# Layer norm in a two-block transformer kernel: the row normalization by ScalarE instead of VectorE

## The chip, the cores and the metric

The kernel runs on one core of a Trainium2 chip, in one launch. The metric is the device time of that launch in microseconds (us). A core has five engines that run side by side and meet only at semaphores: TensorE (PE in the profile; PEld is its weight load), VectorE (DVE), ScalarE (ACT), GpSimd (POOL) and SyncE (SP, which issues most of the DMAs). Each engine takes its own instructions in program order.

## The reference, cut to what matters

Two blocks of two layers each work on 256 tokens of 1024 features in float32. In the first block each layer is a mixer and an MLP, and each of these four sublayers ends in a layer norm, whose rows feed the next projection:

```
def layer_norm(x, g, b):
    mu = mean(x, -1);  var = mean(square(x - mu), -1)
    return (x - mu) * rsqrt(var + 1e-5) * g + b

for layer in range(2):
    shift, scale, gate = ada_modulation(c, ada_w[layer, 0], ada_b[layer, 0])
    h = x * (1 + scale) + shift
    y = mixer(h)                                   # layer 0: windowed + sparse, layer 1: block attention
    x = layer_norm(ALPHA * x + gate * y, ln_g[layer, 0], ln_b[layer, 0])
    shift, scale, gate = ada_modulation(c, ada_w[layer, 1], ada_b[layer, 1])
    h = x * (1 + scale) + shift
    y = square(relu(h @ w1)) @ w2
    x = layer_norm(ALPHA * x + gate * y, ln_g[layer, 1], ln_b[layer, 1])
```

The second block (neighbourhood attention, full attention, a per-layer gate, RMS norms) has no layer norm.

## The kernel before, in words

The 256 tokens lie as T = 2 tiles of 128 rows, called t = 0 and t = 1. A weight tile is 128 x 2048 floats (1 MB) and lands in one of five slots `raw`. Each product is done in a split form: ScalarE rounds the tile to the high part `w_hi` (L1293, three slots, plus `w_spare`), VectorE subtracts to get the low part `w_lo` (L1851, written over `raw`), and TensorE does three matmuls per chunk, with `w_lo`, `w_hi` and the low part of the activations. The activations are split likewise into `ht_hi` and `ht_lo`. ScalarE's and VectorE's parts of a weight tile are issued some tiles ahead (`split_high`, `split_low`, up to `it["ahead"]`).

A function `make_plan` writes one list of items by hand, and all engines walk through this list in the same order, each doing its share of an item. So the place of an item in the list is its place in every engine's queue that has a share in it. A DMA into a `raw` slot waits for the `tile_done` of the tile that was there.

A layer norm of sublayer s is made so, once for each t (item `ln`, from `norm_ln(s, t)`):
- VectorE's eviction of the last projection (`y_ln`, L2109 to L2112) adds gate and residual into `u` and takes statistics, in two column halves.
- `ln` on VectorE (L2137 to L2140): aggregate, add eps, a reciprocal square root in nine one-column instructions (`rsqrt_one`, L1872 to L1877), and then L2140, which normalizes all 1024 columns of `u[:, t, :]` in place and raises `rows_ready`.
- TensorE transposes the rows (item `turn_rows` of the next sublayer, from `across`, L1684) once `rows_ready` allows it. The transposed rows get gain, norm bias and modulation in one step by ScalarE (L1357) and are rounded to `ht_hi` (L1361), then VectorE takes `ht_lo` (L1856). For the second half of t = 1 VectorE does all of it (L2066, L2070, L1856).

Around a layer norm the list reads, in `entered` (before an MLP; s is the MLP's number, so its norm is s - 1) and in `halves` (before a mixer's projections) alike:

```
norm_ln(s - 1, 0)                    # placed before the last projection tiles of t = 1
across(s, 0, ...)                    # transposes of t = 0
norm_ln(s - 1, 1)
ada_tiles(2, 7)                      # in halves it stands before norm_ln(s - 1, 1)
part(0, 0) or first(0, 1, ts=(0,))   # first weight tile of the next projection, t = 0; ahead = 1
across(s, 1, ...)                    # transposes of t = 1
part(0, 1) or first(1, 0, ts=(0,))   # second weight tile, t = 0
```

So there are four such places (norms 0 to 3), with one `ln` of t = 0 and one of t = 1 in each. The item after `ln` of t = 1 carries, on ScalarE and VectorE, the split of the second weight tile.

Of the kernel before, what the change touches and what calls it, by code (L numbers as in the profile page):

```python
# [33 lines left out]
ALU = mybir.AluOpType  # L34
ACT = mybir.ActivationFunctionType
AX = mybir.AxisListType.X

P = 128
S = 256
T = S // P  # L40
# [902 lines left out]
def block_kernel(nc, R, out, toeplitz):  # L943
# [3 lines left out]
    with ExitStack() as ctx:  # L947
        def sb(name, shape, dt=F32):
            return ctx.enter_context(nc.sbuf_tensor(name, shape, dt))

        def sem(name):
            return ctx.enter_context(nc.semaphore(name))
# [3 lines left out]
        u = sb("u", [P, T, D])  # L956
# [23 lines left out]
        gain = sb("gain", [P, 2, HD])  # L980
        stats = sb("stats", [P, T, 2, 6])
        meanvar = sb("meanvar", [P, T, 2])
        ssq = sb("ssq", [P, T, 2])
        rms = sb("rms", [P, 4, 2, T])
        small = sb("small", [P, 3, 24])
        bits = sb("bits", [P, 24], U32)
        rstd = sb("rstd", [P, 24])
# [66 lines left out]
        squares_ready = sem("squares_ready")  # L1054
        key_squares = sem("key_squares")
        rows_ready = sem("rows_ready")
        silu_ready = sem("silu_ready")
        early_affine = sem("early_affine")
        affine_ready = sem("affine_ready")
# [90 lines left out]
        def head_cols(mode, t):  # L1150

            return P * (t + 1) if mode in ("causal", "window", "sparse", "index") else S
# [5 lines left out]
        def turned_view(mode, p2):  # L1158

            n = P * len(turned_blocks(mode))  # L1160
            return probs_t[:, p2, :, :].rearrange("p b s -> p (b s)")[:, 0:n], n
# [107 lines left out]
        def _(act):  # L1269
# [25 lines left out]
            def squares(t, n):  # L1295
                nc.scalar.activation(junk[:, :], x[:, t, n * 512:(n + 1) * 512], ACT.Square,
                                     accum_out=ssq[:, t, n:n + 1]).then_inc(ssq_ready, 1)
                squared[0] += 1
                act.wait_ge(ssq_ready, squared[0])
# [9 lines left out]
            for it in plan:  # L1309
                kind = it["kind"]  # L1310
# [38 lines left out]
                elif kind == "turn_rows" and it["engine"] == "act":  # L1349
# [5 lines left out]
                    for c in range(4):  # L1355
                        k = it["a"] + c
                        ins = nc.scalar.activation(full[:, b % 4, c * P:(c + 1) * P], bank[b][:, c * P:(c + 1) * P], ACT.Identity,  # L1357
                                                   scale=aff[:, it["s"], 0, k:k + 1], bias=aff[:, it["s"], 1, k:k + 1])
# [28 lines left out]
                elif kind in ("tokens", "hidden", "up_tokens", "turn_hidden", "evict"):  # L1387
# [24 lines left out]
                    elif end[0] in ("tok", "silu"):  # L1412
                        c0, scale, width = end[1:4]
# [38 lines left out]
                elif kind == "resid" and it["s"] == 3 and it["t"] == T - 1:  # L1452
                    for t in range(T):
                        act.wait_ge(first_rows, T + t + 1)
                        for n in range(2):
                            squares(t, n)

                elif kind == "index":
                    for j in range(2):
                        b, _ = it["banks"][j]  # L1460
                        act.wait_ge(index_scores, 2 * it["p"] + j + 1)
                        if it["p"]:
                            act.wait_ge(index_used, 2 * it["p"] + j - 1)
                        for t in range(T):
                            m = head_cols("index", t)
                            ins = nc.scalar.activation(biased[:, j, t, 0:m], bank[b][:, t * S:t * S + m], ACT.Relu)
                        ins.then_inc(bank_free[b], 1)

                elif kind == "scores":
                    mode, g = it["mode"], it["g"]  # L1470
                    for j in range(2):
                        b, _ = it["banks"][j]
                        r = g % PAIRS_HELD
                        if mode == "window":
                            act.wait_ge(band_ready, g + 1)
                        else:
                            act.wait_ge(negmax_ready, 2 * (g - BANDED) + j + 1)
                        if g >= 2:
                            act.wait_ge(probs_turned, 2 * (g - 2) + j + 1)
                        if mode == "window":  # L1480
                            hh = it["heads"][j][4]
                            nc.scalar.activation(sink_exp[:, r, :, j], nmx[:, r, :, j], ACT.Exp, bias=sinks[:, 0, hh:hh + 1])
                        for t in range(T):
                            m = head_cols(mode, t)
                            src = biased[:, j, t, :] if mode == "near" else bank[b][:, t * S:t * S + m]
                            by = q_norm[:, t, it["heads"][j][4]:it["heads"][j][4] + 1] if mode == "full" else -1.0
                            ins = nc.scalar.activation(probs[:, g % 2, j, t, 0:m], src, ACT.Exp, bias=nmx[:, r, t, j:j + 1], scale=by,
                                                       accum_out=sums[:, r, t, j:j + 1])
                        ins.then_inc(probs_ready if mode == "near" else bank_free[b], 1)

                elif kind == "split_out":
                    act.wait_ge(tile_done, it["projected"] + 1)
                    for b, used in it["after"]:
                        act.wait_ge(bank_free[b], used)
                    a = it["a"]
                    nc.scalar.activation(ht_hi[:, a:a + 2, :], out_turned[:, a:a + 2, :], ACT.Copy).then_inc(high_copied, 1)

                elif kind == "values" and it["mode"] in TURNED_OUT:
                    b, _ = it["banks"][0]
                    act.wait_ge(head_out, 2 * it["g"] + 2)  # L1500
                    nc.scalar.activation(out_turned[:, it["heads"][0][4] // 2, :], bank[b][:, 0:S], ACT.Copy).then_inc(bank_free[b], 1)

                elif kind == "scale" and it["mode"] in NORMED_BY_SCALAR:
                    g = it["g"]
                    act.wait_ge(sums_turned, g + 1)
                    for j in range(2):
                        for t in range(T):
                            rows = probs[:, g % 2, j, t, 0:head_cols(it["mode"], t)]
                            ins = nc.scalar.activation(rows, rows, ACT.Copy, scale=rs[:, g % PAIRS_HELD, t, j:j + 1])
                        ins.then_inc(normed, 1)  # L1510

                elif kind == "probs":
                    g = it["g"]
                    for j in range(2):
                        b, _ = it["banks"][j]
                        act.wait_ge(probs_turned, 2 * g + j + 1)
                        if g >= 1:
                            act.wait_ge(head_out, 2 * g + j - 1)
                        dst, n = turned_view(it["mode"], j)
                        nc.scalar.activation(dst, bank[b][:, 0:n], ACT.Copy).then_inc(bank_free[b], 1)  # L1520
# [299 lines left out]
        def _(dve):  # L1820
            steps = [0]

            def link(ins):

                steps[0] += 1
                ins.then_inc(dve_step, 1)
                dve.wait_ge(dve_step, steps[0])
# [41 lines left out]
            def rsqrt_one(y, v):  # L1869

                t = small[:, 1, 0:1]
                link(nc.vector.tensor_scalar(bits[:, 0:1], v.bitcast(U32), 1, None, ALU.logical_shift_right))  # L1872
                link(nc.vector.tensor_scalar(y.bitcast(U32), bits[:, 0:1], -1.0, RSQRT_MAGIC, ALU.mult, ALU.add))
                for less in (3.0, 12.0, 768.0):
                    link(nc.vector.scalar_tensor_tensor(t, y, v, y, ALU.mult, ALU.mult))
                    link(nc.vector.scalar_tensor_tensor(y, t, -less, y, ALU.add, ALU.mult))
                link(nc.vector.tensor_scalar(y, y, -1.0 / 8192, None, ALU.mult))  # L1877
# [59 lines left out]
            for it in plan:  # L1937
                kind = it["kind"]
# [34 lines left out]
                elif kind == "columns":  # L1973
# [4 lines left out]
                    bias = vec[:, 3 * KD * it["s"] + at:3 * KD * it["s"] + at + KD]  # L1978
                    dst, src = mod[:, it["s"], at:at + KD], bank[b][:, 0:KD]
                    if it["how"] == "rows":  # L1980
                        dst, bias = (v.rearrange("p (c i) -> p i c", c=2) for v in (dst, bias))
# [153 lines left out]
                elif kind == "ln":  # L2135
                    t = it["t"]
                    link(nc.vector.bn_aggr(meanvar[:, t, :], stats[:, t, :, :]))  # L2137
                    link(nc.vector.tensor_scalar(small[:, 0, 0:1], meanvar[:, t, 1:2], LN_EPS, None, ALU.add))
                    rsqrt_one(rstd[:, 0:1], small[:, 0, 0:1])
                    nc.vector.tensor_scalar(u[:, t, :], u[:, t, :], meanvar[:, t, 0:1], rstd[:, 0:1], ALU.subtract, ALU.mult).then_inc(rows_ready, 1)  # L2140
                    dve.wait_ge(rows_ready, it["rows"])

                elif kind == "resid":

                    t = it["t"]
# [117 lines left out]
                elif kind == "topk":  # L2263

                    for r in range(it["first"], it["first"] + 4):
                        t = r // 8
# [58 lines left out]
                elif kind == "scale":  # L2325
# [10 lines left out]
                    for j in range(2):  # L2336
                        for t in range(T):
                            rows = probs[:, g % 2, j, t, 0:head_cols(mode, t)]
# [75 lines left out]
```

## Time and profile before

| | |
|---|---|
| median of 3 runs (lowest, highest) | 1054.5 us (1053.75, 1055.5) |
| the profiled execution: its time, its span | 1052.61 us, 1050.8 us |
| TensorE busy, its mean granted clock | 978.2 us (93%), 0.98 of full speed |
| VectorE busy | 720.1 us (69%) |
| ScalarE busy | 543.6 us (52%) |
| GpSimd busy | 49.2 us (5%) |
| DMA | 204.85 MB, mean 195 GB/s |
| the chain that ended last, by engine | PE 66%, DVE 17%, ACT 7%, DMA 6%, issue 3% |

The span runs from the first to the last instruction; the time has 1.8 us around it. Busy time is that of matmuls whose ends are modelled. "Issue" is time in which the profile shows nothing that was waited for. In a timeline a row is: start in us, duration in us, engine, line, operation, output <- inputs, shape, count, and in brackets the idle time before it with what ended it.

### The profile page before, as it was taken

The numbers are of one execution on the slowest core, as the hardware profiler recorded it, in microseconds if no ns is written. First come the engines' busy times: TensorE is split into PE (matmuls) and PEld (weight loads), VectorE is DVE, ScalarE is ACT, GpSimd is POOL, SyncE is SP. The second block draws the span as 40 slices with busy tenths as digits, with TensorE's granted clock in tenths as the row PEclk, the third lists the DMA queues.
The fourth block names the chain that finished last, engine by engine and source line by source line (L and its number), as shares of the span: only waits on it lengthen the run. The fifth ranks groups of instructions, "written<-read, shape, count | busy, mean of one in ns | idle before, by whom it ended". The sixth has DMA issues, their size and how long they took to land.

```text
span 1050.8 us, 14669 instructions
## 1 busy us (share of the span) xinstructions
PE 978.2 (93%) x5692; PEld 792.5 (75%) x5692; DVE 720.1 (69%) x1113; ACT 543.6 (52%) x869; POOL 49.2 (5%) x39
## 2 busy tenths in 40 slices
PE   6886998999999989999899999989999999998995
PEld 2663666989898866777699989877788887875684
DVE  3488668777776587565885554478654778797775
ACT  3367725544453253555355455435565746656662
POOL 0000003200000000000071100000000000000000
PEclk9999999999999989999999999999999999999998
DMA  9747476879897468332689776554434346551041
GB/s 350 245 145 295 161 240 214 287 258 341 298 328 261 160 238 294 127 118 64 200 269 254 209 234 188 183 190 132 149 121 130 121 141 200 187 174 61 32 160 40
DMA packets 106931, 204.85 MB, mean 195 GB/s; under 512 B 3488, under 2 KB 37680, under 8 KB 106864
## 3 DMA queue, kind: packets, MB, share of 16 engines
q1 hardware_dynamic: 103808, 193.25, 54.8%
q0 software_dynamic: 3056, 10.67, 3.5%
q8 instruction: 46, 0.75, 0.3%
q14 instruction: 21, 0.17, 0.0%
HBM read 202.76 MB, written 1.15 MB: 194 GB/s over the span
## 4 chain that ended last, share of the span: by engine, by line
PE 66%; DVE 17%; ACT 7%; DMA 6%; issue 3%; SPq 1%; ACTq 0%; DVEq 0%
PE bank L1672 13%; PE bank L1674 13%; PE bank L1673 13%; DVE w_lo L1851 5%; PE bank L1726 5%; PE bank L1728 4%; PE bank L1727 4%; DMA raw<-in_mlp_w 3%; PE bank L1747 2%; ACT w_hi L1293 2%; PE bank L1769 2%; DMA raw<-in_ada_w 2%; DMA raw<-in_ab_w_in 1%; PE bank L1574 1%; PE bank L1814 1%
## 5 line engine op out<-in xcount | busy, mean ns | idle before, releaser
L1851 DVE TENSOR_TENSOR w_lo<-raw,w_hi 128x2048 fp32r<-128x2048 f32 (+2 forms) x134 | 308.6, 2311 | 154.5 <-ACT w_hi L1293 153.4
L1293 ACT ACTIVATE w_hi<-raw 128x2048 fp32r<-128x2048 f32 (+2 forms) x134 | 248.5, 1857 | 131.3 <-PE bank L1674 69.2
L1672 PE MATMUL bank<-w_lo,ht_hi 128*128 128x512 f32 (+1 forms) x544 | 218.4, 401 | 12.5 <-DVE w_lo L1851 7.8
L1674 PE MATMUL bank<-w_hi,ht_lo 128*128 128x512 f32 (+1 forms) x528 | 206.4, 391 | 0.0
L1673 PE MATMUL bank<-w_hi,ht_hi 128*128 128x512 f32 (+1 forms) x528 | 206.1, 390 | 0.0
L1672 PEld LDWEIGHTS bank<-w_lo,ht_hi 128*128 128x128 f32 x544 | 103.7, 191 | 41.8 <-issue 21.4
L1726 PE MATMUL bank<-ht_hi,w_lo 128*128 128x256 f32 x448 | 127.5, 285 | 2.4 <-DVE w_lo L1851 2.4
L1727 PE MATMUL bank<-ht_lo,w_hi 128*128 128x256 f32 x448 | 126.8, 283 | 0.0
L1728 PE MATMUL bank<-ht_hi,w_hi 128*128 128x256 f32 x448 | 126.8, 283 | 0.0
L1674 PEld LDWEIGHTS bank<-w_hi,ht_lo 128*128 128x128 f32 x528 | 100.5, 190 | 21.3
L1673 PEld LDWEIGHTS bank<-w_hi,ht_hi 128*128 128x128 f32 x528 | 101.0, 191 | 18.8
L1672 PE MATMUL bank<-w_lo,hid_hi 128*128 128x512 f32 x256 | 102.0, 399 | 0.0
L1673 PE MATMUL bank<-w_hi,hid_hi 128*128 128x512 f32 x240 | 94.6, 394 | 0.0
L1674 PE MATMUL bank<-w_hi,hid_lo 128*128 128x512 f32 x240 | 94.4, 393 | 0.0
L1726 PEld LDWEIGHTS bank<-ht_hi,w_lo 128*128 128x128 f32 x448 | 85.9, 192 | 5.1 <-issue 5.0
L1727 PEld LDWEIGHTS bank<-ht_lo,w_hi 128*128 128x128 f32 x448 | 86.0, 192 | 0.2
L1728 PEld LDWEIGHTS bank<-ht_hi,w_hi 128*128 128x128 f32 x448 | 86.0, 192 | 0.0
L1672 PEld LDWEIGHTS bank<-w_lo,hid_hi 128*128 128x128 f32 x256 | 48.8, 191 | 10.5 <-issue 0.5
L1357 ACT ACTIVATE full<-bank,aff 128x128 f32<-128x128 f32 x48 | 18.0, 455 | 71.0 <-PE bank L1684 71.0
L1673 PEld LDWEIGHTS bank<-w_hi,hid_hi 128*128 128x128 f32 x240 | 45.9, 191 | 9.9 <-issue 0.5
L1674 PEld LDWEIGHTS bank<-w_hi,hid_lo 128*128 128x128 f32 x240 | 45.8, 191 | 9.7
L1856 DVE TENSOR_TENSOR hid_lo<-full,hid_hi 128x512 fp32r<-128x512 f32 x32 | 24.1, 760 | 33.5 <-ACT hid_hi L1410 33.4
(244 smaller groups left out, 1334.2 us busy)
## 6 DMA issues: line engine op xcount, KB each, us to landing
raw<-in_mlp_w SPq DMA_DIRECT2D x64, 1024.0 KB, 6.0
raw<-in_ada_w SPq DMA_DIRECT2D x44, 1024.0 KB, 5.3
raw<-in_a_w_in SPq DMA_DIRECT2D x16, 1024.0 KB, 5.3
raw<-in_c_w_in SPq DMA_DIRECT2D x12, 1024.0 KB, 5.4
raw<-in_b_w_in SPq DMA_DIRECT2D x10, 1024.0 KB, 5.1
raw<-in_ple_w_gate SPq DMA_DIRECT2D x8, 1024.0 KB, 5.0
raw<-in_ab_w_in SPq DMA_DIRECT2D x4, 1024.0 KB, 9.8
tok<-in_ada_w SPq DMA_DIRECT2D x4, 1024.0 KB, 12.8
```

What stands on the lines that cost most here:

```text
L1293: nc.scalar.activation(split_parts(n)[0], raw_tile(t), ACT.Copy).then_inc(high_done, 1)
L1357: ins = nc.scalar.activation(full[:, b % 4, c * P:(c + 1) * P], bank[b][:, c * P:(c + 1) * P], ACT.Identity, scale=aff[:, it["s"], 0, k:k ...
L1672: nc.tensor.matmul(dst, a_hi[:, c, rows], lo[:, k, :], start=it["first"] and k == 0, stop=False)
L1673: nc.tensor.matmul(dst, a_hi[:, c, rows], hi[:, k, :], start=False, stop=False)
L1674: mm = nc.tensor.matmul(dst, a_lo[:, c, rows], hi[:, k, :], start=False, stop=it["last"] and k == it["kc"] - 1)
L1726: nc.tensor.matmul(dst, lo[:, k, cols], ht_hi[:, k, :], start=k == 0, stop=False)
L1727: nc.tensor.matmul(dst, hi[:, k, cols], ht_lo[:, k, :], start=False, stop=False)
L1728: mm = nc.tensor.matmul(dst, hi[:, k, cols], ht_hi[:, k, :], start=False, stop=k == KD - 1)
L1747: done.append(nc.tensor.matmul(bank[b][:, t * S:t * S + m], qkt[part, qc, t * P:(t + 1) * P], qkt[part, kc, 0:m], start=True, stop=not masks))
L1769: mm = nc.tensor.transpose(bank[b][:, i * P:(i + 1) * P], probs[:, g % 2, j, t, k * P:(k + 1) * P], ident)
L1851: nc.vector.tensor_tensor(lo, raw_tile(split[n]), hi.bitcast(F32), ALU.subtract).then_inc(low_done, 1)
L1856: nc.vector.tensor_tensor(lo, v, hi.bitcast(F32), ALU.subtract).then_inc(split_done, 1)
```

## The change

VectorE no longer normalizes the rows. After the reciprocal square root, which now has a column of `rstd` for each t, it computes `less` = -(mean x rstd), one value per token, and raises a new semaphore `norm_ready`. ScalarE gets a share in the item `ln`: it waits for `norm_ready` and computes `u` = rstd x `u` + `less` in place, as one activation (Identity) with a scale and a bias per partition, and raises `rows_ready`. The list is the same.

```
@@ ScalarE
+                elif kind == "ln":
+                    t = it["t"]
+                    act.wait_ge(norm_ready, T * it["s"] + t + 1)
+                    nc.scalar.activation(u[:, t, :], u[:, t, :], ACT.Identity, scale=rstd[:, t:t + 1], bias=less[:, t, :]).then_inc(rows_ready, 1)
@@ VectorE
                     link(nc.vector.bn_aggr(meanvar[:, t, :], stats[:, t, :, :]))
                     link(nc.vector.tensor_scalar(small[:, 0, 0:1], meanvar[:, t, 1:2], LN_EPS, None, ALU.add))
-                    rsqrt_one(rstd[:, 0:1], small[:, 0, 0:1])
-                    nc.vector.tensor_scalar(u[:, t, :], u[:, t, :], meanvar[:, t, 0:1], rstd[:, 0:1], ALU.subtract, ALU.mult).then_inc(rows_ready, 1)
-                    dve.wait_ge(rows_ready, it["rows"])
+                    rsqrt_one(rstd[:, t:t + 1], small[:, 0, 0:1])
+                    nc.vector.scalar_tensor_tensor(less[:, t, :], meanvar[:, t, 0:1], -1.0, rstd[:, t:t + 1], ALU.mult, ALU.mult).then_inc(norm_ready, 1)
+                    dve.wait_ge(norm_ready, T * it["s"] + t + 1)
```

ScalarE's queue at the first layer norm (s = 0), before. The four L1357 and the L1361 handle transposed rows, `w_hi` is the split of a weight tile:

```order
L1293 ACTIVATE w_hi<-raw 128x2048 [waits tile_done,raw_in2]
L1357 ACTIVATE full<-bank,aff 128x128 [waits split_done,affine_ready,job_done]
L1357 ACTIVATE full<-bank,aff 128x128 x3
L1361 ACTIVATE ht_hi<-full 128x4x128 [waits bank_free4]
L1357 ACTIVATE full<-bank,aff 128x128 [waits split_done,affine_ready,job_done]
L1357 ACTIVATE full<-bank,aff 128x128 x3
L1361 ACTIVATE ht_hi<-full 128x4x128 [waits bank_free5]
L1293 ACTIVATE w_hi<-raw 128x2048 [waits tile_done,raw_in4]
L1357 ACTIVATE full<-bank,aff 128x128 [waits split_done,affine_ready,job_done]
```

The same place in the changed kernel:

```order
L1295 ACTIVATE w_hi<-raw 128x2048 [waits tile_done,raw_in2]
L1496 ACTIVATE u<-u,less,rstd 128x1024 [waits norm_ready]
L1359 ACTIVATE full<-bank,aff 128x128 [waits split_done,affine_ready,job_done]
L1359 ACTIVATE full<-bank,aff 128x128 x3
L1363 ACTIVATE ht_hi<-full 128x4x128 [waits bank_free4]
L1359 ACTIVATE full<-bank,aff 128x128 [waits split_done,affine_ready,job_done]
L1359 ACTIVATE full<-bank,aff 128x128 x3
L1363 ACTIVATE ht_hi<-full 128x4x128 [waits bank_free5]
L1496 ACTIVATE u<-u,less,rstd 128x1024 [waits norm_ready]
L1295 ACTIVATE w_hi<-raw 128x2048 [waits tile_done,raw_in4]
L1359 ACTIVATE full<-bank,aff 128x128 [waits split_done,affine_ready,job_done]
```

Two instructions are new, one for each t; the second stands ahead of a `w_hi` which the transposed rows of t = 1 follow. The other three layer norms read the same.

VectorE's queue at the `ln` of t = 1 of the same norm, before:

```order
L1877 TENSOR_SCALAR rstd<-rstd 128x1 [waits dve_step]
L2140 TENSOR_SCALAR u<-u,meanvar,rstd 128x1024 [waits dve_step]
L1851 TENSOR_TENSOR w_lo<-raw,w_hi 128x2048 [waits high_done,rows_ready]
L1856 TENSOR_TENSOR ht_lo<-full,ht_hi 128x4x128 [waits high_copied]
L2066 TENSOR_SCALAR full<-bank,aff 128x128 [waits job_done]
```

And in the changed kernel:

```order
L1884 TENSOR_SCALAR rstd<-rstd 128x1 [waits dve_step]
L2147 SCALAR_TENSOR_TENSOR less<-meanvar,rstd 128x1 [waits dve_step]
L1858 TENSOR_TENSOR w_lo<-raw,w_hi 128x2048 [waits high_done,norm_ready]
L1863 TENSOR_TENSOR ht_lo<-full,ht_hi 128x4x128 [waits high_copied]
L2073 TENSOR_SCALAR full<-bank,aff 128x128 [waits job_done]
```

One instruction takes the place of another there; nothing is moved. TensorE's, GpSimd's and SyncE's queues hold the same instructions in the same order.

## Rows read from the trace of the kernel before

**Rows 1.** Part 1 of the page: busy us, share, instructions.

```profile
PE 978.2 (93%) x5692; PEld 792.5 (75%) x5692; DVE 720.1 (69%) x1113; ACT 543.6 (52%) x869; POOL 49.2 (5%) x39
```

**Rows 2.** Waits: who for whom, us in total, times, longest.

```profile
PE bank L1684 <- DVE u L2140: 4.4, 6, 2.1
...
PE bank L1698 <- DVE w_lo L1851: 1.7, 2, 1.2
```

**Rows 3.** Timeline of VectorE at the first norm.

```profile
160.41 0.81 DVE L2140 TENSOR_SCALAR u<-u,meanvar,rstd 128x1024 f32<-128x1024 f32 x1
...
165.62 1.37 DVE L1856 TENSOR_TENSOR ht_lo<-full,ht_hi 128x512 fp32r<-128x512 f32 x2
...
169.06 0.15 DVE L1877 TENSOR_SCALAR rstd<-rstd 128x1 f32<-128x1 f32 x1
169.25 0.81 DVE L2140 TENSOR_SCALAR u<-u,meanvar,rstd 128x1024 f32<-128x1024 f32 x1
170.09 2.29 DVE L1851 TENSOR_TENSOR w_lo<-raw,w_hi 128x2048 fp32r<-128x2048 f32 x1
```

**Rows 4.** Timeline of ScalarE at the first norm.

```profile
165.63 0.63 ACT L1361 ACTIVATE ht_hi<-full 128x512 fp32r<-128x512 f32 x1
166.17 1.90 ACT L1293 ACTIVATE w_hi<-raw 128x2048 fp32r<-128x2048 f32 x1
170.87 1.50 ACT L1357 ACTIVATE full<-bank,aff 128x128 f32<-128x128 f32 x4 [2.81 <-PE bank L1684]
...
177.11 0.60 ACT L1396 ACTIVATE biased<-bank 128x512 f32<-128x512 f32 x1 [4.07 <-PE bank L1700]
```

**Rows 5.** Timeline of TensorE at the first norm.

```profile
161.37 1.07 PE L1684 MATMUL bank<-consts,u 128*128 128x128 f32 x8 [0.15 <-DVE u L2140]
...
172.44 0.38 PE L1698 MATMUL bank<-w_lo,ht_hi 128*128 128x256 f32 x1 [1.17 <-DVE w_lo L1851]
```

**Rows 6.** The chain that ended last, at the second norm: start, us, what.

```profile
377.87 2.30 DVE w_lo L1851
...
381.08 0.43 PE bank L1673
...
385.10 0.23 PE bank L1674
```

**Rows 7.** Timeline at the third norm: ScalarE, TensorE, ScalarE.

```profile
513.99 1.90 ACT L1293 ACTIVATE w_hi<-raw 128x2048 fp32r<-128x2048 f32 x1
...
520.26 0.39 PE L1698 MATMUL bank<-w_lo,ht_hi 128*128 128x256 f32 x1 [0.49 <-DVE w_lo L1851]
...
523.44 0.60 ACT L1396 ACTIVATE biased<-bank 128x512 f32<-128x512 f32 x1 [1.91 <-PE bank L1700]
```

**Rows 8.** Timeline at the fourth norm: VectorE twice, TensorE.

```profile
711.32 2.29 DVE L1851 TENSOR_TENSOR w_lo<-raw,w_hi 128x2048 fp32r<-128x2048 f32 x1
...
714.81 0.69 DVE L1856 TENSOR_TENSOR ht_lo<-full,ht_hi 128x512 fp32r<-128x512 f32 x1 [1.20 <-ACT ht_hi L1361]
...
734.41 0.47 PE L1672 MATMUL bank<-w_lo,ht_hi 128*128 128x512 f32 x1 [1.38 <-DVE w_lo L1851]
```

**Rows 9.** ScalarE's groups by form: busy us, mean ns, idle before.

```profile
L1293 ACT ACTIVATE w_hi<-raw 128x1024 fp32r<-128x1024 f32 x6 | 6.3, 1052 | 0.1
...
L1338 ACT ACTIVATE full<-bank 128x256 f32<-128x256 f32 x8 | 2.6, 383 | 7.2 <-PE bank L1638 7.1
...
L1340 ACT ACTIVATE full<-bank,aff 128x256 f32<-128x256 f32 x4 | 2.0, 554 | 0.2 <-PE bank L1638 0.2
```

**Rows 10.** Instructions of two of VectorE's lines: ns least/median/most.

```profile
L2140 DVE TENSOR_SCALAR u<-u,meanvar,rstd x8: 811/812/815, 160.4 to 710.5; 128x1024 f32<-128x1024 f32 x8
...
L1876 DVE SCALAR_TENSOR_TENSOR rstd<-small,rstd x24: 159/159/161, 159.1 to 710.1; 128x1 f32<-128x1 f32 x24
```

**Rows 11.** Stretches: busy us of PE, PEld, DVE, ACT, POOL; PEclk; DMA share, GB/s.

```profile
173.00:175.00 2.00, 2.00 (x12) 2.00 (x11) 1.93 (x5) 0.04 (x1) 0.00 (x0) 0.51 0.46 162
...
177.00:179.00 2.00, 2.00 (x19) 2.00 (x18) 0.00 (x0) 1.89 (x2) 1.92 (x2) 1.00 0.00 0
...
521.00:523.00 2.00, 2.00 (x19) 2.00 (x19) 1.44 (x4) 0.53 (x1) 0.00 (x0) 1.00 0.29 113
```

More of the change, by code:

```diff
@@ L982, in block_kernel @@
         meanvar = sb("meanvar", [P, T, 2])
+        less = sb("less", [P, T, 1])
         ssq = sb("ssq", [P, T, 2])
@@ L1056, in block_kernel @@
         rows_ready = sem("rows_ready")
+        norm_ready = sem("norm_ready")
         silu_ready = sem("silu_ready")
```

## The prediction

> **What bounds the kernel now.** I read the page's busy line first: TensorE is busy 93% of the span, so time is lost only where TensorE stands, or where it is late and cannot catch up [rows 1]. Then I looked at the waits: the transposes waited for the normalized rows 4.4 us in six instances, and the first matmuls on the second weight tile of an MLP waited for `w_lo` twice [rows 2]. Both happen at the layer norms. So the total for VectorE (69%) is no guide; the four places where a layer norm ends are. I read the timelines of the three engines at the first norm, and the chain or the timeline at the others.
>
> At the first norm, t = 0: VectorE normalizes at 160.41, TensorE transposes at 161.37, 0.15 us after its end [rows 3, 5]. ScalarE rounds the second half of these rows until 166.26, and VectorE's second `ht_lo` starts at 166.3, right behind that; from there VectorE runs without a gap through the small instructions of t = 1 to the normalization at 169.25 and to `w_lo` at 170.09 [rows 3, 4]. That `w_lo` ends at 172.38, and TensorE, idle for 1.17 us, starts on it at 172.44 [rows 3, 5]. ScalarE made the `w_hi` for it at 166.17 to 168.07, while VectorE was still on the statistics, and then had nothing to do for 2.81 us [rows 4]. That is the pattern to keep in mind: VectorE's chain is the one that ends last, and ScalarE runs 2 us ahead of it. At the second norm the chain of waits itself goes through this `w_lo` (377.87) into the matmuls [rows 6]; the third has TensorE waiting 0.49 us for it at 520.26 [rows 7].
>
> **The change, part by part.**
>
> What goes: eight VectorE instructions of 812 ns (L2140) [rows 10].
>
> What comes on VectorE: eight one-column instructions with one tensor and one constant operand. L1876 is of that kind, 159 ns [rows 10]. With 0.03 us to the next instruction, VectorE is free 0.65 us earlier each time.
>
> What comes on ScalarE: eight activations of 1024 columns with scale and bias from memory. The trace has none. From below it is the plain copy of 1024 columns, 1052 ns; adding scale and bias from memory costs 171 ns at 256 columns (554 against 383, both from PSUM) [rows 9]. If that addition grew with the columns it would be 684 ns, so the upper bound is 1.74 us. I take 1052 + 171 = 1223 ns, since such an addition looks like a fixed cost of two reads.
>
> The skill speaks against this move: the Trainium skill, "ScalarE: Activation LUTs", "Rules for kernel authors", gives add and multiply to VectorE and keeps ScalarE for functions that only it has. The rows of both engines agree: 812 ns is measured and 1.22 us is the sum above [rows 9, 10]. By that rule alone one would write down 8 x 0.4 us = 3.3 us, for the duration only; the placing below costs more.
>
> Rows ready later: before, from the end of `rstd` to the end of L2140 it is 0.03 + 0.81 = 0.84 us (169.21 to 170.06) [rows 3]. After: 0.03 + 0.16 for `less`, some 0.04 for the hop to ScalarE, 1.22 for the activation, 1.45 in all. Each set of normalized rows is 0.61 us later.
>
> t = 0, four times. ScalarE's new instruction stands behind `w_hi` work long done, and what is behind it waits for the transposes anyway. VectorE's gain of 0.65 us goes unused: its next step that matters, the second `ht_lo`, already waits for ScalarE's rounding (166.26 against 166.3) [rows 3, 4], and that moves by 0.61. At the first and third norm the first `ht_lo` may start up to 0.6 us earlier, and so TensorE on its first chunk, but the second half of the chunks waits for the second `ht_lo`. So t = 1's chain on VectorE starts 0.61 us later. That is the first term, and it is carried into the next.
>
> t = 1, four times. Here the new instruction stands on ScalarE's queue ahead of the `w_hi` of the second weight tile. Before, this `w_hi` ran during VectorE's small instructions (166.17, 513.99) [rows 4, 7]; now it is held behind an instruction that waits for their result. Before, from the end of `rstd` to the start of `w_lo`: 169.21 to 170.09, 0.88 us [rows 3]. After: 0.03 + 0.16 + 0.04 + 1.22, then `w_hi` of 1.90, which overlaps its predecessor by 0.1 (166.17 against 165.63 + 0.63 = 166.26) [rows 4], and 0.03 to VectorE: 3.28 us. The difference is 2.4 us. With the 0.61 carried, `w_lo` and the matmuls on it start 3.0 us later. The transposed rows of t = 1 are behind the same `w_hi` on ScalarE: its L1357 moves from 170.87 to about 173.1, and their `ht_lo` on VectorE waits for the late `w_lo`; both are done before TensorE has finished the 24 matmuls on the second tile, so they add nothing at the first three norms.
>
> Nothing gives the 3.0 us back there. TensorE is at work almost without a gap afterwards [rows 1], and the next weight DMAs wait for `tile_done`, so they move along; in the stretch from 177 to 179 us the DMA share is 0.00, because all slots are full [rows 11]. First, second and third norm: 3 x 3.0 = 9.1 us.
>
> At the fourth norm the first catch-up follows at 734.41, where TensorE waits 1.38 us for a VectorE `w_lo` that hangs on the residual update and the RMS norm [rows 8]. VectorE's chain to there starts with the `ht_lo` at 714.81. The late `w_lo` (711.32 + 3.0, 2.2 us from start to start) puts it at 716.6, 1.8 us later [rows 8]. TensorE's own lateness of 3.0 eats the 1.38 us of idle time (1.6 are left), so the chain decides: 1.8 us.
>
> Sum: 9.1 + 1.8 = 10.9 us.
>
> TensorE's clock. At the first norm the granted clock was 0.51 from 173 to 175 us, the lower level of 1.2 GHz, after a stretch with idle time, and back at 1.00 (2.4 GHz) from 177 on [rows 11]. The 24 matmuls on the second tile took 172.44 to 177.11, 4.67 us; at the third norm, at full clock [rows 11], 520.26 to 523.44, 3.18 us [rows 4, 5, 7]. At the second norm a 512-column matmul took 0.43 us at the low level against 0.23 later [rows 6]. The change adds 3 us of idle time ahead of just these matmuls. Bounds: from below, the low stretches keep their place in time and fall into the idle time, which gives back the 1.5 us of the first norm and 12 x 0.2 = 2.4 us of the second, -4 us. From above, the third norm's 24 matmuls run low, +1.5 to 2.2, the fourth's 12 matmuls too, +2.4, and the first and second stay low 0.5 to 1 us longer, +6 us. I take +1.5, nearer to the upper rows, since the idle time gets longer in all four places.
>
> "TensorE: Matmul & The Clock Gate" in the Trainium skill, Part 1, says it so: "the default state is throttled, and activity releases the throttle". By it the low stretches would begin again after the longer idle and the sum would be the upper one; that the clock fell after idle time agrees [rows 11].
>
> The sum against the profiled execution: 1052.6 + 10.9 + 1.5 = 1065.0 us. That execution lies 1.9 us under the median of the runs (1054.5), so the median after comes out at 1066.9, or 1067.
>
> **The rivals.**
>
> 1. `w_hi` is not decisive: only the later rows count. For: ScalarE has idle time here, and TensorE might have other work. Then the transposes of t = 1 are 0.61 + 0.61 = 1.2 us late, four times: 4.9 us, 1059.4. Against: the queue shows `w_hi` behind the new instruction, and the matmuls started 0.06 us after `w_lo` [rows 3, 5].
>
> 2. The clock takes its upper bound: 10.9 + 6 = 16.9 us, 1071 (with an activation at its upper bound, 8 x 0.5 more on the same path, 1075).
>
> 3. The other side: VectorE's relief shows. The place is the small chain of t = 1 and the `w_lo` behind it, the price 8 x 0.65 = 5.2 us, the time 1049.3. It decides only from the point where ScalarE's activation and the held `w_hi` end before VectorE would have reached its `w_lo`, that is, if ScalarE needed less than 0.65 us for both. 1.90 us for `w_hi` alone speaks against it [rows 4].
>
> 4. The clock takes its lower bound, 10.9 - 4 = 6.9 us, 1061.4.
>
> **How the numbers follow.** Forecast (3.0 us at three norms, 1.8 at the fourth, clock between 0 and +3.5): 0.6. Rival 1: 0.1. Rival 2: 0.16. Rival 3: 0.03. Rival 4: 0.11. 0.2%, or 2.1 us, is about what a measurement of this kernel can tell from no change; all cases but the third lie beyond it. Faster 0.03, same 0.02, slower 0.95. The range takes in most of rivals 2 and 4: 1061 to 1073 us.
>
> **What the profile after would show.** ScalarE's eight new activations near 1.22 us. At each norm's t = 1 ScalarE's order activation, `w_hi`, `full`, with `w_hi` at about 171.3 at the first norm, VectorE idle some 3 us ahead of `w_lo` for ScalarE's `w_hi`, and TensorE's first matmul on it near 175.4 instead of 172.44. The same shift of about 3 us at the second and third norm, and from the fourth on a total of 10 to 13 us. The sum is wrong if TensorE starts on that tile less than 2 us later, or if the shift shrinks again between two norms. The clock term shows in the granted clock just after these starts.

## The result, and the profile after

The changed kernel takes 1071.0 us (median of 4 runs, 1064.9 to 1071.8), the kernel before 1054.1 us (median of 4): the ratio is 1.0165, 95% interval 1.0133 to 1.0197. It is slower by 17 us; the forecast was 1067 us, between 1061 and 1073. The profiled execution took 1071.4 us, its span is 1069.6 us.

Part 1 of its page, which answers to [rows 1], and two groups of its part 5 (line, engine, operation, tiles, count | busy us, mean ns | idle before, and what ended it):

```profile
PE 984.3 (92%) x5692; PEld 796.8 (74%) x5692; DVE 709.4 (66%) x1113; ACT 553.0 (52%) x877; POOL 45.7 (4%) x39
...
L1858 DVE TENSOR_TENSOR w_lo<-raw,w_hi 128x2048 fp32r<-128x2048 f32 (+2 forms) x134 | 305.9, 2290 | 182.0 <-ACT w_hi L1295 181.0
...
L1496 ACT ACTIVATE u<-u,less,rstd 128x1024 f32<-128x1024 f32 x8 | 9.9, 1241 | 67.1 <-DVE less L2147 67.1
```

VectorE has 10.7 us less to do (5.2 of it are the exchanged instructions, 8 x 0.65; the rest is in instructions that were not changed) and ScalarE 9.4 us more, and the kernel is 17 us longer: the work is not what counts. VectorE's idle time ahead of `w_lo` for ScalarE's `w_hi` grew from 153.4 to 181.0 us. The waits of the changed kernel, against [rows 2]:

```profile
PE bank L1691 <- ACT u L1496: 12.4, 8, 2.7
...
PE bank L1705 <- DVE w_lo L1858: 6.1, 2, 3.0
```

The waits of the transposes for the rows grew from 4.4 to 12.4 us, those for `w_lo` at the two MLPs from 1.7 to 6.1 us.

The first norm, VectorE (timeline, as [rows 3]):

```profile
160.06 0.16 DVE L2147 SCALAR_TENSOR_TENSOR less<-meanvar,rstd 128x1 f32<-128x1 f32 x1
...
166.56 0.69 DVE L1863 TENSOR_TENSOR ht_lo<-full,ht_hi 128x512 fp32r<-128x512 f32 x1 [1.26 <-ACT ht_hi L1363]
...
169.51 0.16 DVE L2147 SCALAR_TENSOR_TENSOR less<-meanvar,rstd 128x1 f32<-128x1 f32 x1
172.85 2.29 DVE L1858 TENSOR_TENSOR w_lo<-raw,w_hi 128x2048 fp32r<-128x2048 f32 x1 [3.18 <-ACT w_hi L1295]
```

ScalarE there, as [rows 4]:

```profile
169.71 1.24 ACT L1496 ACTIVATE u<-u,less,rstd 128x1024 f32<-128x1024 f32 x1 [3.17 <-DVE less L2147]
170.85 1.90 ACT L1295 ACTIVATE w_hi<-raw 128x2048 fp32r<-128x2048 f32 x1
172.66 1.48 ACT L1359 ACTIVATE full<-bank,aff 128x128 f32<-128x128 f32 x4
```

TensorE there, as [rows 5]:

```profile
171.09 1.06 PE L1691 MATMUL bank<-consts,u 128*128 128x128 f32 x8 [2.08 <-ACT u L1496]
175.20 0.58 PE L1705 MATMUL bank<-w_lo,ht_hi 128*128 128x256 f32 x1 [3.04 <-DVE w_lo L1858]
```

Read the three together: ScalarE stands idle for 3.17 us with a finished weight tile waiting in `raw`, because the instruction at the head of its queue waits for VectorE; then VectorE stands idle 3.18 us for the `w_hi` that was held; then TensorE 3.04 us for the `w_lo`.

To compare the norms I take the time from the first instruction after the reciprocal square root of t = 0 (L2140 before, `less` after) to TensorE's first matmul on the second weight tile. At the first norm it was 160.41 to 172.44, 12.03 us [rows 3, 5], and is 160.06 to 175.20, 15.14 us: 3.11 us more. At the second, third and fourth norm the changed kernel has 373.35 to 388.57, 517.40 to 532.53 and 715.63 to 730.85; before it was 368.20 to 380.31, 508.24 to 520.26 and 701.65 to 713.75. The differences are 3.11, 3.11 and 3.12.

From norm to norm the changed kernel falls behind by 5.5, 4.0 and 4.8 us, and by 4.8 us more from the fourth norm to the end. So 3.1 us of each step are the late second tile, and the rest comes after it.

Most of the rest is TensorE's clock. Stretches of the changed kernel, columns as in [rows 11], around those starts:

```profile
173.00:175.00 2.00, 0.00 (x0) 0.00 (x0) 2.00 (x1) 1.77 (x5) 0.00 (x0) 0.50 0.69 243
175.00:177.00 2.00, 1.80 (x8) 1.80 (x9) 2.00 (x6) 0.00 (x0) 0.00 (x0) 0.50 0.00 0
177.00:179.00 2.00, 2.00 (x12) 2.00 (x11) 1.14 (x3) 0.00 (x0) 0.64 (x1) 0.50 0.00 0
532.00:534.00 2.00, 1.47 (x7) 1.47 (x8) 2.00 (x6) 0.13 (x1) 0.00 (x0) 0.50 0.04 14
534.00:536.00 2.00, 2.00 (x11) 2.00 (x11) 1.47 (x4) 0.00 (x0) 0.31 (x1) 0.50 0.00 0
```

The granted clock is 0.50 while the second tile of the first and of the third norm runs. At the third norm it was at 1.00 before [rows 11]; the 24 matmuls that took 3.18 us there now take 532.53 to 538.06, 5.5 us. The mean clock of the whole execution fell from 0.980 to 0.970; span and clock of the changed kernel:

```profile
core 0: 1069.6 us, clock 0.970
```

At half speed a loss of 0.01 is 2% of the span, so TensorE spent about 42 us at the lower level before (2 x 0.020 x 1050.8) and 64 us now. Its busy time says the same in another way: with the same 5692 matmuls it grew from 978.2 to 984.3 us, by 6.1, and the idle time from 72.6 to 85.3 us, by 12.7. As an estimate from these two executions, some 6 of the 18.8 us between them are slower matmuls and some 13 are waits.

### The profile page after: what moved, and what is told of

It is laid out like the page before. It is cut to its first block, busy times and chain, and to the rows that moved or that the text cites. A ratio compares the mean times of both kernels' runs of the same rounds, so it can differ in the third digit from the quotient of the medians.

```text
span 1069.6 us, 14677 instructions
## 1 busy us (share of the span) xinstructions
PE 984.3 (92%) x5692; PEld 796.8 (74%) x5692; DVE 709.4 (66%) x1113; ACT 553.0 (52%) x877; POOL 45.7 (4%) x39
## 4 chain that ended last, share of the span: by engine, by line
PE 66%; DVE 15%; ACT 8%; DMA 5%; issue 4%; SPq 1%; ACTq 0%; DVEq 0%
PE bank L1679 13%; PE bank L1681 13%; PE bank L1680 13%; DVE w_lo L1858 4%; PE bank L1733 4%; PE bank L1735 4%; PE bank L1734 4%; ACT w_hi L1295 3%; DMA raw<-in_mlp_w 3%; PE bank L1754 2%; PE bank L1776 2%; DMA raw<-in_ab_w_in 1%; DMA raw<-in_ada_w 1%; PE bank L1581 1%; PE bank L1821 1%
## 5 line engine op out<-in xcount | busy, mean ns | idle before, releaser
L1858 DVE TENSOR_TENSOR w_lo<-raw,w_hi 128x2048 fp32r<-128x2048 f32 (+2 forms) x134 | 305.9, 2290 | 182.0 <-ACT w_hi L1295 181.0
L1754 PE MATMUL bank<-qkt 64*128 64x256 f32 (+1 forms) x288 | 40.7, 383 | 6.2 <-ACT probs L1489 2.9
L1496 ACT ACTIVATE u<-u,less,rstd 128x1024 f32<-128x1024 f32 x8 | 9.9, 1241 | 67.1 <-DVE less L2147 67.1
```

Of the source, the lines that this page charges most:

```text
L1754: done.append(nc.tensor.matmul(bank[b][:, t * S:t * S + m], qkt[part, qc, t * P:(t + 1) * P], qkt[part, kc, 0:m], start=True, stop=not masks))
L1858: nc.vector.tensor_tensor(lo, raw_tile(split[n]), hi.bitcast(F32), ALU.subtract).then_inc(low_done, 1)
```

## The experiments

Each run was timed against the kernel before on the same chip. Single runs of the kernel before differ by 8 to 13 us within one such comparison, so the ratios with their intervals count, not the medians alone.

**Split first.** One thing is changed in the changed kernel: ScalarE's `w_hi` goes ahead of the normalization of t = 1.

```
@@ ScalarE
                 elif kind == "ln":
                     t = it["t"]
+                    if t == 1:
+                        after = plan[plan.index(it) + 1:]
+                        split_high(next(i["ahead"] for i in after if "ahead" in i))
                     act.wait_ge(norm_ready, T * it["s"] + t + 1)
```

> The changed kernel with one thing moved: at the normalization of t = 1 ScalarE first makes the w_hi of the second weight tile, then the normalization. Theory A (the held w_hi is what costs): w_hi runs during VectorE's small instructions again, VectorE's w_lo follows its new one-column instruction and starts within 0.2 us of where it was before the change; TensorE's first matmul on the second tile is less than 0.5 us later than before at each norm, the transposed rows of t = 1 some 1 us later, which costs 0 to 1 us a norm; 1054 to 1059 us. Rival B (the rows that are ready later are what costs): the shift of about 3 us at each norm stays, 1064 to 1071 us. Theory C (most of it is TensorE's clock): between the two, and the granted clock stays at 0.97.

Measured: ratio 1.0007 (0.9981 to 1.0033), median 1053.4 us against 1052.3; mean clock 0.982. The whole loss is gone although ScalarE does the same eight activations. Timeline of ScalarE at the first norm, which starts some 2 us later in this execution:

```profile
168.34 1.90 ACT L1295 ACTIVATE w_hi<-raw 128x2048 fp32r<-128x2048 f32 x1
171.61 1.24 ACT L1499 ACTIVATE u<-u,less,rstd 128x1024 f32<-128x1024 f32 x1 [1.37 <-DVE less L2150]
```

TensorE there:

```profile
172.99 1.06 PE L1694 MATMUL bank<-consts,u 128*128 128x128 f32 x8 [2.08 <-ACT u L1499]
...
179.08 0.39 PE L1708 MATMUL bank<-w_lo,ht_hi 128*128 128x256 f32 x1 [0.55 <-DVE ht_lo L1866]
```

And VectorE there:

```profile
171.61 2.29 DVE L1861 TENSOR_TENSOR w_lo<-raw,w_hi 128x2048 fp32r<-128x2048 f32 x1
175.86 0.69 DVE L1866 TENSOR_TENSOR ht_lo<-full,ht_hi 128x512 fp32r<-128x512 f32 x1 [1.97 <-ACT ht_hi L1363]
```

VectorE's `w_lo` and ScalarE's activation now start at the same moment, 171.61, and `w_lo` waits for nothing. The transposes still waited 2.08 us for the rows, as long as in the changed kernel, and it cost nothing: that wait lies under `w_lo`. From `less` of t = 0 to the second tile it is 11.99, 12.08, 11.99 and 12.62 us at the four norms, against 12.03, 12.11, 12.02 and 12.10 before the change. Two effects cancel in it: the second half's chain still starts 0.62 us later (9.45 us from `less` to `less`, against 8.83 from `u` to `u`), and VectorE is free 0.65 us earlier. The new wait is the 0.55 us of TensorE for the `ht_lo` of t = 1, inside the 0 to 1 us expected. Theory A holds, but for the 0.52 us of the fourth norm, where less than 0.5 was expected; rival B falls.

**Hold only.** The kernel before; no work is moved, ScalarE only waits.

```
@@ ScalarE
+                elif kind == "ln" and it["t"] == 1:
+                    act.wait_ge(rows_ready, it["rows"])
```

> The kernel before, VectorE normalizes everything; only ScalarE waits for the normalized rows of t = 1 ahead of the w_hi of the second weight tile. No work is moved. Theory A: w_hi starts at VectorE's end of the normalization and takes 1.9 us, so w_lo and TensorE's first matmul on it are 1.9 us later at the first three norms and about 0.5 to 1 at the fourth: 6.5 us, with the clock's part 1 to 5 us more: 1061 to 1066 us. Rival B (the activation itself and the later rows cost): no change, 1054 us.

Measured: ratio 1.0095 (1.006 to 1.013), +10 us, median 1061.4; mean clock 0.975. Timeline of ScalarE at the first norm, where `u` of t = 0 starts at 160.98:

```profile
170.66 1.91 ACT L1293 ACTIVATE w_hi<-raw 128x2048 fp32r<-128x2048 f32 x1 [3.82 <-DVE u L2143]
```

VectorE there:

```profile
172.67 2.29 DVE L1854 TENSOR_TENSOR w_lo<-raw,w_hi 128x2048 fp32r<-128x2048 f32 x1 [2.05 <-ACT w_hi L1293]
```

From `u` to TensorE's first matmul on the second tile (175.01) it is 14.03 us against 12.03, 2.0 us more, and so it is at the other three norms (14.13, 14.03 and 14.12 us). A wait without any work costs 10 us (6 to 14), more than half of the 17.

**Only one of the two halves.** In both kernels the other half is normalized by VectorE as before.

```
@@ ScalarE
-                elif kind == "ln":
+                elif kind == "ln" and it["t"] == 0:        # in the second kernel: == 1
                     t = it["t"]
-                    act.wait_ge(norm_ready, T * it["s"] + t + 1)
+                    act.wait_ge(norm_ready, it["s"] + 1)
...
@@ VectorE, behind rsqrt_one
+                    if t != 0:                             # in the second kernel: != 1
+                        nc.vector.tensor_scalar(u[:, t, :], u[:, t, :], meanvar[:, t, 0:1], rstd[:, t:t + 1], ALU.subtract, ALU.mult).then_inc(rows_ready, 1)
+                        dve.wait_ge(rows_ready, it["rows"])
+                        continue
```

> ScalarE normalizes the rows of t = 0 only, VectorE those of t = 1 as before the change. Theory A: the second ht_lo of t = 0 is 0.6 us later and carries 0.6 us through VectorE's chain into the second weight tile, at four norms: 2.4 us, 1055.5 to 1058.5 us. Rival B (both halves cost alike): half of the 17 us, 1062 us. Theory C (any added idle time of TensorE tips its clock): over 1060 us, with the clock under 0.975.

> ScalarE normalizes the rows of t = 1 only, VectorE those of t = 0 as before the change. Theory A: 2.4 us at each of the first three norms and about 1.2 at the fourth, 8.4 us, and with the clock's part some 3 to 6 us more: 1064 to 1069 us. Rival B (both halves cost alike): 1062 us, the same as with t = 0 only. If the clock's part needs the full 3 us of a norm: about 1063 us.

Measured: t = 0 only 1.0032 (1.0007 to 1.0057), +3.4 us; t = 1 only 1.0132 (1.0086 to 1.0178), +13.9 us. With t = 0 only, VectorE's `less` to TensorE's second tile is 12.65 us at the first norm (159.54 to 172.19), 0.6 more than before, as in the sum. With t = 1 only, the same distance is 14.52 us (163.86 to 178.38), 2.5 more, where 2.4 was in the sum, and the mean clock is 0.970, as low as in the changed kernel. Together the two losses give 17.3 us, the whole, though each has an interval of some us. "Both halves cost alike" is out, and so is the theory that any idle time tips the clock: the first kernel's mean clock was 0.979.

**Useless matmuls in TensorE's waits.** To take the clock out I gave TensorE bf16 matmuls of constants into an empty bank where it waits; they change no result. The kernel before and the changed one, filled (the edit is cut to its parts):

```
+            def fill(at, n):
+                held = next(i["banks"] for i in plan[at + 1:] if i["kind"] in ("tokens", "up_tokens"))
+                b, used = held[1]
+                if used:
+                    pe.wait_ge(bank_free[b], used)
+                for _ in range(n):
+                    nc.tensor.matmul(bank[b][:, 0:3 * P], maskb[:, 0, :], maskb[:, :, :].rearrange("p a n -> p (a n)"), start=True, stop=True)
...
+                if kind == "up_tokens" and it["t"] == 0 and it["h"] == 0:
+                    fill(at - 1, 6)                        # 4 in the changed kernel
+                if kind == "turn_rows" and it["t"] == 1 and it["a"] == 0:
+                    fill(at, 3)                            # 8
...
+                    if it["t"] == 1 and it["a"] == 4:      # behind the transposes
+                        fill(at, 5)                        # 14
```

> The kernel before with useless matmuls (bf16, 384 columns, into an empty bank, of constants) where TensorE waits at each layer norm: 6 ahead of the first projection tile of an MLP, 3 ahead of the transposes of t = 1, 5 behind them. They take 0.16 us each at full clock and lie in waits of 1.7, 0.7 and 1.2 us. Clock theory: the low stretches at the four norms (173, 378, 514 and 706 us) go away or get shorter, and with them up to half of 3.4, 6.8, 3.4 and 6.8 us: 1044 to 1052 us. Rival (the clock costs nothing that the waits would not): no change or up to 2 us slower.

> The changed kernel with the same useless matmuls, 4 ahead of the first projection tile of an MLP, 8 ahead of the transposes of t = 1, 14 behind them. Clock theory: the waits for w_hi and w_lo stay (3 us at three norms, 2 at the fourth), the low stretches at the norms go: TensorE's first matmul on the second tile 3 us later than in the filled kernel before, and the two filled kernels differ by 9 to 12 us instead of 17; 1056 to 1065 us. Rival (all of the 17 us is the waits): 1069 to 1072 us.

Measured: the kernel before, filled, 0.9972 (0.9943 to 1.0001), median 1048.5 us; the changed kernel, filled, 1.0078 (1.0052 to 1.0104), median 1059.3. The first interval just reaches no change. Both have a mean clock of 0.984. The useless matmuls moved no wait at the second tile: at the first norm it is 12.03 us from `u` to it in the filled kernel before (160.42 to 172.45) and 15.14 from `less` in the filled changed one (161.21 to 176.35), as without them. Timeline of TensorE at the first norm of the filled changed kernel:

```profile
173.15 2.44 PE L1545 MATMUL bank<-maskb 128*128 128x384 bf16 x14
...
176.35 0.39 PE L1720 MATMUL bank<-w_lo,ht_hi 128*128 128x256 f32 x1 [0.77 <-DVE w_lo L1873]
```

The stretches of that kernel that follow, columns as in [rows 11]:

```profile
176.00:178.00 2.00, 1.65 (x13) 1.65 (x14) 2.00 (x6) 0.00 (x0) 0.00 (x0) 1.00 0.01 4
178.00:180.00 2.00, 2.00 (x19) 2.00 (x18) 1.29 (x3) 0.47 (x1) 0.49 (x1) 1.00 0.00 0
```

`w_lo` (174.00 there) ends no earlier and ScalarE's hold is unchanged (VectorE idle 3.18 us for `w_hi` again), but the clock stays at 1.00 here. (At the fourth norm, from 711 to 717 us, it is low in this kernel too.) With the mean clock equal, the change costs 1.0078 / 0.9972 = 1.0106, 11 us (from the two intervals about 7 to 15). Without the useless matmuls it costs 17. So about 11 us are waits, and about 6 are the clock that falls with them. The 6 are a difference of two differences: by the intervals they may be anything from 1 to 11 us. That TensorE's busy time grew by 6.1 us between the two unfilled profiles is the second hint at this size. I had expected the filled pair to differ by 9 to 12 us; it did.

**Versions that might beat both.** VectorE normalizes t = 0, ScalarE t = 1 with `w_hi` ahead of it (the edits of "split first" and of t = 1 only together):

> t = 0 normalized by VectorE, t = 1 by ScalarE with w_hi ahead of it. By theory A nothing is later for t = 0, and VectorE reaches its w_lo 0.65 us earlier at each norm, which moves TensorE's second tile up by 0.5 us: 1 to 2 us faster than before, 1050.5 to 1053 us, unless the transposed rows of t = 1, 0.6 us later, take its place: then 1053 to 1055 us. Rival (ScalarE's share costs as such): over 1056 us.

Measured: 1.0014 (0.9993 to 1.0035): no gain. At the first norm VectorE did reach its `w_lo` 9.02 us after `u` of t = 0 (162.07 to 171.09) instead of 9.68, 0.66 earlier. But TensorE then waited 0.55 us for the `ht_lo` of t = 1 (at 178.57), as in the first experiment: the later transposed rows took the gain back, the outcome named second.

The changed kernel with `w_hi` first, filled:

> The changed kernel with w_hi ahead of the normalization on ScalarE, and useless matmuls (5, 8 and 3). The w_hi theory and the clock theory together: as the filled kernel before, within 2 us (1044 to 1054 us). Rival: as the unfilled one with w_hi first, 1053 us.

Measured: 1.0009 (0.9986 to 1.0032), median 1053.9 us: not what I expected of the two theories together, the rival's figure instead. At the first norm its clock was at 1.00 from 170 to 180 us, as meant; its mean clock is 0.981 all the same, against 0.984 for the filled kernel before. Its low stretches lie at 317 to 323, 351 to 357, 706 to 712 and 737 to 740 us; why they are longer there I did not find out. Here the useless matmuls are also in the way: from `less` to the second tile it is 12.29 us at the first norm and 13.30 at the fourth, against 11.99 and 12.62 without them. At the fourth norm the eight ahead of the transposes take from 712.19 to 713.69 us, and the transposes follow them without a gap.

The kernel before with more filling, a plan item with 10 useless matmuls at the fourth norm added (`add("fill", bank=6, used=uses[6], n=10)` ahead of `norm_ln(s - 1, 1)` in `halves`), and the version with t = 1 on ScalarE, filled:

> The kernel before with more useless matmuls: 8, 3 and 5 at the places of the filled kernel before, and 10 at the fourth norm between the transposes of t = 0 and the first projection, where TensorE waits 2.7 us. Clock theory: the low stretch of 6.8 us at the fourth norm goes too, 1 to 2 us below the filled kernel: 1045 to 1050 us. Rival: the low stretches left come from elsewhere, as the filled one, 1048.5 us.

> t = 0 by VectorE, t = 1 by ScalarE with w_hi ahead of it, with useless matmuls (8, 4, 3 and 10). If both theories add: TensorE's second tile 0.6 us earlier at each norm than in the filled kernel before, 0 to 2 us faster than that: 1044 to 1049 us. Rival: the later transposed rows of t = 1 take back the gain, as the filled kernel before or 1 us slower, 1047 to 1051 us.

Measured: the kernel before with more filling 0.9952 (0.9929 to 0.9975), median 1048.6 us, mean clock 0.986, and at 1.00 from 706 to 712 us, where the fourth norm had its low stretch. The version with t = 1 on ScalarE 0.9971 (0.9943 to 1.0), median 1052.0 us, above both ranges set down for it; its runs went from 1044 to 1056 us. The first is the only kernel of this study that is clearly faster than the kernel before, by 5 us. Against the first filled kernel (0.9972) its further gain is within the intervals. That ScalarE's share adds something on top is not shown.

## Why the prediction was right

The direction and the mechanism were right, and so was the size of the waits at three of the four norms; the size of the clock's term was not. What was measured is rival 2's figure, 1071, and not the forecast's 1067 with a clock between 0 and +3.5 us. The range holds it because it was drawn wide enough to take in rival 2.

- **The activation.** 1223 ns were summed, 1241 ns measured in all eight. Since its successor starts 1.14 us after it (169.71, 170.85), the path pays less.
- **Later rows, t = 0.** 0.61 us forecast. The second `ht_lo` is 6.50 us behind `less` (166.56 - 160.06) against 5.9 behind `u` before, 0.6. Alone it costs 3.4 us in four norms, 2.4 forecast, and the interval (0.7 to 6) holds both. VectorE's relief was not used, as forecast: it stood idle 1.26 us for ScalarE's rounding instead.
- **The held `w_hi`.** 3.0 us a norm forecast with the carried part, 3.11 measured four times. From `less` of t = 1 to `w_lo` it is 3.34 us (169.51 to 172.85), 3.25 in the sum. The experiment that puts `w_hi` back ahead removes the loss, and the wait without work brings back 2.0 us a norm. "Nothing gives the 3.0 us back" did not quite hold: some 10 us after the first norm's second tile TensorE had waited 0.75 us before (183.57) and does not wait now (185.82), and its lateness falls from 3.2 to 2.3 us.
- **The transposed rows of t = 1** add nothing at the first norms: L1359 at 172.66 was forecast at 173.1.
- **The fourth norm.** 1.8 us were forecast for it without the clock, and 4.5 came with it: the first instruction of the norm starts 13.98 us later than before (715.63 against 701.65), the catch-up matmul 18.44 (752.85 against 734.41 [rows 8]). VectorE's chain moved as forecast: the `ht_lo` of t = 1 is 15.8 us late (730.62 against 714.81), 1.8 more than the norm. But the chain did not decide. At its third `w_lo` from there VectorE had to wait for ScalarE, which had waited 6.87 us for TensorE before it could start on that `w_hi` (at 739.03). And TensorE had started on the late second tile at 730.85 and run at the low clock until 736. VectorE, then TensorE:

```profile
741.05 2.29 DVE L1858 TENSOR_TENSOR w_lo<-raw,w_hi 128x2048 fp32r<-128x2048 f32 x1 [2.68 <-ACT w_hi L1295]
...
752.85 0.47 PE L1679 MATMUL bank<-w_lo,ht_hi 128*128 128x512 f32 x1 [0.32 <-DVE w_lo L1858]
```

Before, the same `w_lo`, at 722.60, waited for nothing. In the filled pair VectorE's wait there is 0.33 us, and from the norm's first instruction to the catch-up it is 34.9 us against 32.3, 2.6 more. So "the chain decides: 1.8" is too small by about 0.8 us without most of the clock's part, and by 2.7 with it.
- **The sum of the waits**, 10.9 us, is met by the filled pair, 11 us (7 to 15). Added up from the traces it would be 3 x 3.1 + 2.6 = 11.9.
- **The clock.** The step that was mis-sized: "I take +1.5, nearer to the upper rows". Measured it is about 6 us, the upper bound that I had worked out and given to rival 2. At the first norm it stayed low longer, at the third it was low while the second tile ran, where it had been at 1.00, and at the fourth it was low during the second tile too. One low stretch was longer already ahead of the second norm (354 to 360 us, against 351 to 354 before), though the profile shows TensorE busy without a gap. Just before it fell there, in both kernels, TensorE ran 32 matmuls of a single column, in the changed one:

```profile
350.86 4.29 PE L1593 MATMUL bank<-consts,late_sum 128*128 128x1 f32 x32
```

No term of mine was about that place; TensorE's lateness grew there from 3.9 us (355.01 against 351.08) to 5.0 (360.28 against 355.24). I took the middle of the bounds, though all four places pointed to the same side. The rule of the Trainium skill that I cited ("TensorE: Matmul & The Clock Gate", Part 1) had named this side. The runs agree with it at the norms, where the waits got longer; at 354 us, where TensorE had no wait, they do not show that longer idle time did it.
- **Rival 1** (only the later rows, 1059) and **rival 3** (VectorE's relief, 1049) fall. In the first experiment the later rows of t = 1 are still there without a loss, and the later rows of t = 0 cost 3.4 us of the 17 when they are alone. VectorE's relief shows only once `w_hi` stands ahead of the normalization: then it pays for the later rows of t = 0, or brings the second tile 0.66 us forward (at the first norm of the version with t = 1 on ScalarE alone). Rival 4 (the clock gives back) did not come as a whole. A small part of it shows at the third norm: before, the clock was low from 514 to 518 us, ahead of the second tile, and in the changed kernel it is not, so TensorE's lateness falls from 8.5 us (522.79 against 514.28) to 7.5 (525.23 against 517.73). On the second tile it grows again, from 12.3 us (532.53 against 520.26) to 14.6 (537.82 against 523.23).

One run of the changed kernel took 1064.9 us, at a mean clock of 0.976; the other three took 1070.7 to 1071.8 at 0.968 to 0.970. In the same program a higher clock thus goes with a shorter run.

## What to carry to other kernels

An instruction that is moved to an engine with idle time can cost more than its duration: it brings its wait along, and all that stands behind it in the queue is held until the wait ends. Before moving, read what follows at the new place and put whatever is ready ahead of it; here the loss of 17 us was gone once that one place in a queue was changed. And when a change makes TensorE wait longer in places where its clock already falls, give the clock's upper bound more weight than its middle; here it was the upper bound that came.

## What the runs showed of the hardware that was not expected

- 44 to 58 useless bf16 matmuls, placed in TensorE's waits, made the kernel before faster by 3 to 5 us (0.9972, whose interval reaches 1.0001, and clearly 0.9952), with the mean granted clock up from 0.980 to 0.984 and 0.986. At the first norm they hold the clock at 1.00 where it was 0.51 from 173 us on. Not every low stretch goes: the filled kernel before is still low from 349 to 355 us, with TensorE busy. The stretches at the first norm of the filled kernel before:

```profile
173.00:175.00 2.00, 2.00 (x19) 2.00 (x18) 1.91 (x5) 0.06 (x1) 0.00 (x0) 1.00 0.52 201
175.00:177.00 2.00, 2.00 (x19) 2.00 (x19) 1.18 (x3) 1.38 (x2) 0.60 (x1) 1.00 0.00 0
```

- An activation of 1024 float32 columns with scale and bias from memory takes 1241 ns, 189 more than the plain copy of 1024 columns and near the 171 ns measured at 256 [rows 9]. By these two pairs the price of scale and bias is fixed; per column it would have been 684 ns.
